# Eighteen places instead of twelve for expert weights, and three experts in one loop body

## The reference

```
logits = xf @ w_router + b_router          # 512 tokens, 32 experts, the best 4 of each token
hu  = xb @ w_gate_up[e] + b_gate_up[e]     # (tokens of e, 1024) @ (1024, 2048)
a   = minimum(hu[:, :1024], 7); lin = clip(hu[:, 1024:], -7, 7)
act = a * sigmoid(1.702 * a) * (lin + 1)
y  += (act @ w_down[e] + b_down[e]) * gate # (tokens of e, 1024) @ (1024, 1024)
```

## Time and profile before

| | |
|---|---|
| median of 3 runs | 1378.53 us (1376.85 to 1381.19) |
| the profiled execution's own time | 1379.79 us |
| its span, first to last instruction | 1377.3 us |
| PE busy | 1325.1 us, 96% of the span |
| bytes moved by DMA | 450.77 MB, mean 327 GB/s |
| granted TensorE clock, mean over the span | 0.981 of full speed |

### The profile page before, as it was taken

One profiled execution on the slowest core, in us unless ns is written; L12 is line 12 of the kernel. 1 busy time (PEld: TensorE's weight loads), 2 busy tenths in 40 slices (PEclk: granted clock), 3 DMA queues, 4 the chain that ended last, 5 costly groups with the idle time before them and its releaser, 6 DMA issues.

```text
span 1377.3 us, 33076 instructions
## 1 busy us (share of the span) xinstructions
PE 1325.1 (96%) x13998; PEld 653.9 (47%) x13998; DVE 498.5 (36%) x887; ACT 205.7 (15%) x313; POOL 272.1 (20%) x260
## 2 busy tenths in 40 slices
PE   6999999988999999999999999999999999999996
PEld 5877667882344444444444444444444433444443
DVE  7465453560333322222233333332222222333324
ACT  5233332230000100000001000010000000110002
POOL 2845236124111111111111111111111111111100
PEclk9999999989999999999999999999999999999998
DMA  9421111665999999999999999999999999999984
GB/s 244 112 57 36 62 61 62 234 260 193 352 382 406 402 409 405 398 408 405 402 404 406 405 395 405 413 408 405 407 406 405 409 408 403 408 406 403 407 355 144
DMA packets 94605, 450.77 MB, mean 327 GB/s; under 512 B 12106, under 2 KB 36954, under 8 KB 45425
## 3 DMA queue, kind: packets, MB, share of 16 engines
q1 hardware_dynamic: 83280, 426.27, 77.4%
q0 software_dynamic: 8656, 19.51, 5.9%
q10 hardware_dynamic: 2640, 4.59, 0.9%
HBM read 440.08 MB, written 18.67 MB: 333 GB/s over the span
## 4 chain that ended last, share of the span: by engine, by line
PE 77%; DMA 9%; DVE 4%; POOL 3%; issue 3%; SPq 2%; ACT 1%; DVEq 0%; POOLq 0%; ACTq 0%
PE gu_bank L1506 40%; PE bank L1520 21%; DMA raw<-in_w_gate_up_dram 9%; PE bank L1285 3%; PE bank L1287 3%; PE bank L1286 3%; PE bank L1494 2%; SPq L383 2%; PE bank L1339 1%; PE bank L1375 1%; ACT probs L727 1%; DVE probs L1018 1%; DVE probs L1005 1%; PE bank L1473 1%; PE bank L1523 1%
## 5 line engine op out<-in xcount | busy, mean ns | idle before, releaser
L1506 PE MATMUL gu_bank<-raw,xT 128*32 128x512 f32 x3072 | 338.2, 592 | 5.0 <-DMA raw<-in_w_gate_up_dram 3.9
L1181 DVE TENSOR_TENSOR gate_in<-gu_bank,b_gu 128x768 f32<-128x768 f32 x32 | 30.6, 958 | 570.9 <-PE gu_bank L1506 540.1
L1506 PEld LDWEIGHTS gu_bank<-raw,xT 128*32 128x32 f32 x3072 | 100.9, 110 | 235.8 <-issue 216.1
L1520 PE MATMUL bank<-raw_a,aT 128*32 128x256 f32 x2232 | 166.8, 380 | 0.0
L1523 PE MATMUL bank<-raw_a,aT 128*32 128x256 f32 x744 | 166.4, 380 | 0.0
L1506 PE MATMUL gu_bank<-raw_c,xT 128*32 128x512 f32 x1488 | 165.5, 592 | 0.0
L585 POOL DMA_INDIRECT sum_rows<-y_out,scatter_list x31 | 45.2, 1457 | 429.8 <-ACT y_out L841 429.8
L1206 DVE STREAM_TRANSPOSE aT<-lin_in 128x192 f32<-128x192 f32 x128 | 68.0, 533 | 143.2 <-PE bank L1523 142.1
L1520 PEld LDWEIGHTS bank<-raw_a,aT 128*32 128x32 f32 x2232 | 88.8, 110 | 62.1
L827 ACT ACTIVATE xT<-bank 128x384 f32<-128x384 f32 x66 | 28.9, 489 | 553.3 <-PE bank L1494 540.3
L1506 PEld LDWEIGHTS gu_bank<-raw_c,xT 128*32 128x32 f32 x1488 | 49.6, 110 | 110.1 <-issue 104.7
(11 more groups left out here) (234 smaller groups left out, 1650.9 us busy)
## 6 DMA issues: line engine op xcount, KB each, us to landing
raw<-in_w_gate_up_dram SPq DMA_DIRECT2D x128, 1024.0 KB
raw_c<-in_w_gate_up_dram SPq DMA_DIRECT2D x62, 1024.0 KB
raw_a<-in_w_down_dram SPq DMA_DIRECT2D x62, 1024.0 KB, 22.3
raw_b<-in_w_gate_up_dram SPq DMA_DIRECT2D x32, 1024.0 KB, 21.0
raw_b<-in_w_down_dram SPq DMA_DIRECT2D x32, 1024.0 KB, 26.5
raw_e<-in_w_gate_up_dram SPq DMA_DIRECT2D x31, 1024.0 KB
raw_d<-in_w_down_dram SPq DMA_DIRECT2D x31, 1024.0 KB
raw<-in_w_in_dram SPq DMA_DIRECT2D x24, 512.0 KB, 5.5
```

The lines of the kernel that those rows point to most:

```text
L1181: dve.tensor_tensor(gate_in[:, :, :], gu_bank[:, :, 0:QUARTER], gate_b, ALU.add)
L1506: ins = pe.matmul(gu_bank[c * GROUP:(c + 1) * GROUP, r, :], xT[:, i, r * GROUP:(r + 1) * GROUP], w[:, c], start=first, stop=last)
L1520: pe.matmul(bank_[c * GROUP:(c + 1) * GROUP, cols], aT[:, k, c * GROUP:(c + 1) * GROUP], w[:, at:at + QUARTER], start=first and r % 2 == 0 ...
```

## The change

Four places are added in the memory of `hi01`/`lo01` (`raw_g`) and two in that of `merged` (`raw_f`), so that RAW is 18. Since 12 chunks of an expert don't divide by 18, the loop body takes three experts (36 chunks, two turns of the ring). The places are met in another order, so the chunks that wait for the front are others. The final sum uses `raw_g` instead of `raw01`, and `token_row` moves to where xn lay, with a wait of POOL for `got_turned`.

```diff
-RAW = 12
+RAW = 18
-BODY = 1
+BODY = 3
@@ tensors
-        token_row, last_pick = overlay(0, ("token_row", [P, SEQ], F32), ("last_pick", [P, SEQ], F32))
+        raw_f = overlay(0, ("raw_f", [P, 2, CHUNK], F32))
+        token_row, last_pick = overlay(57 * K, ("token_row", [P, SEQ], F32), ("last_pick", [P, SEQ], F32))
@@ raw_slot
-            for ring in (raw01, raw_a, raw_d, raw_b, raw_e, raw_c):
+            for ring in (raw01, raw_a, raw_d, raw_f, raw_b, raw_g, raw_e, raw_c):
@@ wait_slot
                 elif m == RAW_FRONT + 2:
                     sp.wait_ge(lists_emptied, 16)
                 elif m == RAW_FRONT + 3:
+                    sp.wait_ge(mT_hi_ready, KD)
+                    sp.wait_ge(mT_lo_ready, KD)
+                elif m == RAW_FRONT + 5:
                     wait_used(sp, N_FRONT - 1)
-                elif m == RAW_FRONT + 5:
+                elif m == RAW_FRONT + 11:
                     sp.wait_ge(ss_1_ready, TT)
-                elif m == RAW_FRONT + 6:
+                elif m == RAW_FRONT + 12:
                     sp.wait_ge(router_ready, TT)
@@ end of sync, scalar and vector: the final sum (6 lines, all alike)
-                sp.dma_start(raw01[:, t, 0:D_MODEL], sum_rows[t * P:(t + 1) * P, :]).then_inc(sum_loaded[t], 16)
+                sp.dma_start(raw_g[:, t, 0:D_MODEL], sum_rows[t * P:(t + 1) * P, :]).then_inc(sum_loaded[t], 16)
@@ gpsimd, ahead of token_row
+            pool.wait_ge(got_turned, 2)
```

More of the change, by code:

```diff
@@ L445, in _ @@
             for t in range(TT):
-                sp.dma_start(raw01[:, t, 0:D_MODEL], sum_rows[t * P:(t + 1) * P, :]).then_inc(sum_loaded[t], 16)
+                sp.dma_start(raw_g[:, t, 0:D_MODEL], sum_rows[t * P:(t + 1) * P, :]).then_inc(sum_loaded[t], 16)
             for t in range(TT):
                 sp.wait_ge(out_ready, t + 1)
-                sp.dma_start(out[0, t * P:(t + 1) * P, :], raw01[:, t, 0:D_MODEL]).then_inc(out_stored, 16)
+                sp.dma_start(out[0, t * P:(t + 1) * P, :], raw_g[:, t, 0:D_MODEL]).then_inc(out_stored, 16)
             sp.wait_ge(out_stored, 16 * TT)
@@ L869, in _ @@
                 act.wait_ge(sum_ready, t + 1)
-                act.activation(raw01[:, t, D_MODEL:2 * D_MODEL], raw01[:, t, 0:D_MODEL], ACT.Square,
+                act.activation(raw_g[:, t, D_MODEL:2 * D_MODEL], raw_g[:, t, 0:D_MODEL], ACT.Square,
                                accum_out=ss_f[:, t:t + 1]).then_inc(ss_f_ready, 1)
@@ L1262, in add_last @@
                 dve.wait_ge(fin_ready, t + 1)
-                row = raw01[:, t, 0:D_MODEL].rearrange("p (two n) -> p two n", two=2)
+                row = raw_g[:, t, 0:D_MODEL].rearrange("p (two n) -> p two n", two=2)
                 dve.tensor_tensor(row, row, fin_bank[:, 2 * t:2 * t + 2, :], ALU.add).then_inc(sum_ready, 1)
@@ L1275, in _ @@
                 dve.wait_ge(rstd_f_ready, t + 1)
-                row = raw01[:, t, 0:D_MODEL]
+                row = raw_g[:, t, 0:D_MODEL]
                 dve.scalar_tensor_tensor(row, row, rstd_f[:, t:t + 1], g_fin_row[:, :], ALU.mult, ALU.mult)\
```

## The result

The changed kernel takes 1445.16 us (median of 4 runs, 1441.01 to 1445.56), the kernel before 1377.94 us beside it: a ratio of 1.047 (1.045 to 1.049), 67 us slower. The prediction had the direction and the mechanism, but 1406 us and a range up to 1438.

A forecast was written before the change was run, and what follows sets the result against it. PE was taken as the bound until about 1116 us, transfers in the last fifth. Ring -5.5, jumps +24 and clock +9 gave +27.5 us; 1379.8 + 27.5 - 1.3 = 1406 us, range 1372 to 1438.

The forecast's parts named there:

- The reserve and the ring: Expert loop: six more places hold enough loaded chunks that PE's weight waits after 1116 us vanish, 5.5 us gained.
- The reload: PE's loop: the 148 KB body doesn't stay, so each of 9 jumps back waits for a program packet; chance 0.67.
- The two chances in three: The estimate that PE's three-job loop body of 148 KB doesn't stay at hand.
- The price of a jump: PE's loop branch: a packet takes 3.6 us, 0.9 covered by queued work, 2.7 lost; nine times, 24 us.
- My low row: Small transfer of the lists, taken as landing after 2.7 us with idle queues; lower basis for a packet's price.
- The row of b_dn: Bias of down, 4 KB among full queues, issued at 449.3 and used at 453.8: 4.5 us, second basis for a packet's price.
- The upper end of 8.3 us: Time of a gather, taken as the highest price for fetching a program packet at a jump.
- The clock: PE after each loop pause: a pause may lower its clock; half of the nine counted, 9 us.
- The front: Ahead of job 0: new loads double ACT's 3.33 us wait for x1's store, 1376.3 us; gain given back or never coming: 0.10.
- The range: Whole kernel: 1372 to 1438 us, holding both signs but leaving out the dearest jumps and a gain beyond 6.5 us.
- the prediction's own upper case, 1465 us: Loop jumps: 8.3 us uncovered at each of nine and every clock loss, +86 us.

The follow-up runs named there:

- the written-out ring of eighteen: The changed kernel with experts 1 to 28 written out ahead of the loop, so no jump back is taken: 1361.52 us, ratio 0.9949 to the kernel before.
- two padded jobs: The kernel before with a loop body of two experts and 30 or 60 unread one-column products behind each job's down: 1534.14 and 1642.11 us.

## Why the prediction was right or wrong

**The reserve and the ring: right.** The waits of the last fifth are gone, 5.5 us. In the changed kernel that is no proof of the ring, since they are gone with twelve places too where PE pauses; the written-out ring of eighteen, without a pause, is the proof.

**The reload: right.** The two chances in three were my estimate: the rows show that a body of 49 KB stays and nothing of what is too long. How the program comes they do show. In the kernel before, 19 of the packets come from 0 to 415, while PE executes 4,872 matmuls and weight loads, 256 for a packet:

```profile
q8 instruction: 19, 0.31, 0.3%
```

With 16 KB a packet that is 64 bytes an instruction, as I had it from the whole program (63). The runs put the limit between 1688 and 1808 instructions; three jobs have 2352. A pass brings eleven packets, about ten were foretold.

**The price of a jump: the step that failed.** The term was 2.7 us for each of nine jumps, 24 us; it measured 5.5 us, 49.7 us. The step that gave it reads "A packet of program needs no engine to issue it but shares full queues, so I take the middle of the first two, 3.6 us". That no engine issues it holds: the pages list the packets of `q8` (20 before, 126 after) and no issue for them. So does the sharing: from 415 to 1410 its 106 packets take 0.7% of the 16 engines' time and the data queues 95.6%. But a packet in full queues takes 3.6 us only to begin; then come 1.1 us for itself and 1.4 us until PE goes on, 6.1 us for the branch, of which some 0.6 us are covered (0.9 predicted). So the step took the time in which a small transfer lands for the time until PE goes on, and averaged a row of full queues with one of emptier ones. My low row, the lists at 2.7 us, was measured at a DMA share of 0.43 (334.4 to 337.1), not in idle queues; even at a share of 0.26 the branch takes 3.5 us and the pause 2.9. The row of b_dn (4.5 us, at a share of 1.01 from 449 to 454) was the nearer one, and still too low. The upper end of 8.3 us held.

**The clock: the second term mis-sized.** I counted half of nine at 1.9 us, 9 us. The 1.9 us are those of job 1: behind PE's pause of 3.44 us the granted clock is 0.64 over 4 us, and its gate_up takes 22.50 us instead of 20.60. For the nine jobs behind the pauses it measured 20.3 us, 1.6 to 3.1 us each. The pause that served as model, 3.44 us, was shorter than those that came. With pauses of 2.9 us on the mean three jobs of nine are slow, with 3.8 to 5.3 us all nine. So most of this error, the number of slow jobs, follows from the first; the price of one, 2.26 us on the mean instead of 1.9, is the other 3.2 us. Length alone doesn't decide it near 3 us: a pause of 2.93 us brought the low clock, one of 3.11 didn't.

**The front: small, and not by that rival's path.** ACT waits 3.75 us instead of 3.33 for the store of x1, but goes on earlier, at 290.68 against 291.11. The gather of job 1's tokens goes out 6.3 us later (314.52 against 308.18), yet PE's pause ahead of job 1 is 3.44 us in both. Job 0's gate_up starts 1.2 us later and takes 0.5 us longer, and so job 1 starts 1.75 us later; whether the new loads do that isn't shown.

**The range.** Its upper end, 1438 us, cut off the dearer jumps; the prediction's own upper case, 1465 us, held 1445. The two errors together, 49.7 - 24 = 25.7 us and 20.3 - 9 = 11.3 us, and 1.75 in the front are nearly all of the 39 us between 1406 and 1445.

## What to carry to other kernels

Before unrolling a loop, count the instructions of the longest engine's body as the trace has them (the 96 gate_up matmuls of a job in this program are 192 executed, with as many loads of weights) and compare with a body that the trace shows to stay: here 1688 stayed, and from 1808 on each jump cost a fetch, a branch of 6.1 us at full queues and of 3.5 us at a DMA share of 0.26. Written-out code cost PE nothing where the transfers had a reserve to pay for its packets (882.81 us busy of 883.00), so if a change needs a body that doesn't fit, write out more, not less. A price for a small transfer has to be read from a row taken under the load that it will meet.

## What the runs showed of the hardware that I had not expected

How far a jump goes outside what is held made no difference: bodies of two padded jobs, three and six all have branches of 5.9 to 6.1 us (medians). And the chips differed at one place whatever the kernel: in job 0, gate_up ran without a gap in the written-out ring, from 312.86 to 333.67,

```profile
312.86 10.51 PE L1518 MATMUL gu_bank<-raw,xT 128*32 128x512 f32 x96 [0.58 <-ACT xT L837]
323.18 5.33 PE L1518 MATMUL gu_bank<-raw_a,xT 128*32 128x512 f32 x48
328.33 2.76 PE L1518 MATMUL gu_bank<-raw_d,xT 128*32 128x512 f32 x24
330.91 2.76 PE L1518 MATMUL gu_bank<-raw_f,xT 128*32 128x512 f32 x24
333.60 0.88 PE L1506 MATMUL bank<-ident,x_got 96*128 96x96 f32 x8
```

but in the kernel before and in the changed kernel on their chip the same product went on until 343.94 and 345.69, with many small idle times ended by nothing that the profile names. It took 20.8 us in each of the eight profiles on two of the chips and 32.9 to 35.3 us in the six others. That is 12 us or more, enough for the difference of the kernel before between chips, 1368 against 1378 us. What stalls PE there stays open.
